# Router of a mixture-of-experts layer taken from the raw residual tile by tile, behind an output projection ordered by column halves

## What is computed

```python
x = x + jnp.einsum('blm,md->bld', y, lw['w_out'])
x = x + moe_ffn(rmsnorm(x, lw['norm_ffn_g']), ...)
...
def moe_ffn(x, wg_r, bg_r, we_r, be_r, w_gu, w_down):
    lg = (xt @ wg_r + bg_r)                      # 4 groups
    gsel = jnp.argmax(lg, axis=-1)
    le = (xt @ we_r + be_r)                      # 32 experts, 8 of each group
    tv, ti = lax.top_k(le_g, TOP_E)              # two of the chosen group
    gate = p_group * jax.nn.softmax(tv, axis=-1)
...
        return (jax.nn.silu(a) * b) @ w_down[e]  # a, b: the halves of xb @ w_gu[e]
```

## Time and profile before

| | us |
|---|---|
| three runs, median (lowest to highest) | 889.68 (887.58 to 890.31) |
| the profiled execution: own time | 888.9 |
| its span in the trace | 887.2 |
| TensorE busy | 744.4 (84%) |
| VectorE busy | 217.6 (25%) |
| DMA, mean rate over the span | 279 GB/s |

### The profile page before, as it was taken

How to read it: one execution, slowest core, us unless ns; L and a number is a source line. 1 busy time by engine, 2 the same in 40 slices (tenths; PEclk the granted TensorE clock), 3 DMA queues, 4 the chain that set the end, 5 groups by cost and what they waited for, 6 DMA issues and landing times.

```text
span 887.2 us, 10055 instructions
## 1 busy us (share of the span) xinstructions
PE 744.4 (84%) x3636; PEld 384.7 (43%) x3636; DVE 217.6 (25%) x546; ACT 138.1 (16%) x338; POOL 187.4 (21%) x186
## 2 busy tenths in 40 slices
PE   3999999979898999829999997878777787787883
PEld 3788688857666645523333332222222222222220
DVE  4331104266749332271111011001010010100110
ACT  4212413013253411101000000000000000000000
POOL 6010000160300000012233332321312313223121
PEclk9999999989997999958999999999999999999998
DMA  9742823020420194477999999999999999999992
GB/s 313 115 148 60 262 106 104 1 72 1 182 106 0 43 425 186 153 277 292 408 409 407 413 410 405 415 407 416 411 411 415 409 413 416 408 416 411 413 417 85
DMA packets 75812, 247.55 MB, mean 279 GB/s; under 512 B 24656, under 2 KB 43999, under 8 KB 51163
## 3 DMA queue, kind: packets, MB, share of 16 engines
q1 hardware_dynamic: 62625, 232.00, 66.2%
q0 software_dynamic: 11776, 8.58, 4.4%
q10 hardware_dynamic: 1378, 6.54, 1.8%
HBM read 240.99 MB, written 24.92 MB: 300 GB/s over the span
## 4 chain that ended last, share of the span: by engine, by line
PE 40%; SPq 29%; DMA 14%; DVE 11%; issue 3%; ACT 2%; POOL 0%; ACTq 0%; DVEq 0%; POOLq 0%
PE bank L1063 37%; SPq L570 20%; SPq L577 9%; DMA reg_b<-in_exp_w_gu 6%; PE bank L1066 3%; DMA reg_a<-in_exp_w_gu 3%; DMA reg_w<-in_exp_w_gu 3%; DMA reg_x<-in_x_prompt 1%; DVE reg_a L1722 1%; DVE reg_y L1973 1%; DVE reg_a L1802 1%; DVE reg_a L1712 1%; DVE reg_x L1712 0%; DVE small L1763 0%; POOL small L673 0%
## 5 line engine op out<-in xcount | busy, mean ns | idle before, releaser
L1063 PE MATMUL bank<-reg_w,reg_y 128*64 128x512 f32 (+2 forms) x512 | 136.8, 585 | 18.4 <-DMA reg_w<-in_exp_w_gu 18.4
L1063 PE MATMUL bank<-reg_a,reg_y 128*64 128x512 f32 x528 | 124.5, 607 | 22.7 <-DMA reg_a<-in_exp_w_gu 16.8
L1063 PE MATMUL bank<-reg_b,reg_y 128*64 128x512 f32 x528 | 123.4, 600 | 22.5 <-DMA reg_b<-in_exp_w_gu 16.8
L1977 DVE TENSOR_TENSOR reg_y<-reg_y,bank 128x256 f32<-128x256 f32 x32 | 13.5, 421 | 418.9 <-ACT reg_y L1046 418.9
L1063 PEld LDWEIGHTS bank<-reg_w,reg_y 128*64 128x64 f32 (+2 forms) x512 | 46.1, 146 | 103.5 <-issue 59.5
L1063 PE MATMUL bank<-reg_b,reg_w 128*128 128x260 f32 x384 | 85.3, 383 | 0.0
L1063 PEld LDWEIGHTS bank<-reg_a,reg_y 128*64 128x64 f32 x528 | 34.3, 138 | 104.2 <-issue 50.5
L1063 PEld LDWEIGHTS bank<-reg_b,reg_y 128*64 128x64 f32 x528 | 34.4, 136 | 102.4 <-issue 56.9
L1063 PEld LDWEIGHTS bank<-reg_b,reg_w 128*128 128x128 f32 x384 | 72.7, 190 | 12.0 <-issue 1.1
L673 POOL TENSOR_TENSOR small<-small 128x1 f32<-128x1 f32 (+4 forms) x18 | 20.2, 1127 | 197.2 <-DVE small L1855 68.1
L739 POOL DMA_INDIRECT out_y_p<-reg_y,reg_q x16 | 25.3, 1582 | 166.5 <-ACT reg_y L1050 166.5
(11 more groups left out here) (341 smaller groups left out, 657.1 us busy)
## 6 DMA issues: line engine op xcount, KB each, us to landing
reg_a<-in_exp_w_gu SPq DMA_DIRECT2D x44, 1024.0 KB, 27.9
reg_b<-in_exp_w_gu SPq DMA_DIRECT2D x44, 1024.0 KB, 28.7
reg_w<-in_exp_w_gu SPq DMA_DIRECT2D x40, 1024.0 KB, 27.9
reg_a<-in_exp_w_down SPq DMA_DIRECT2D x22, 1024.0 KB, 28.4
reg_b<-in_exp_w_down SPq DMA_DIRECT2D x22, 1024.0 KB, 28.1
reg_h<-in_exp_w_down SPq DMA_DIRECT2D x20, 1024.0 KB, 28.3
reg_w<-in_w_in SPq DMA_DIRECT2D x9, 1024.0 KB, 10.6
reg_w<-in_w_out SPq DMA_DIRECT2D x1, 4096.0 KB, 13.3
```

The lines of the kernel that those rows point to most:

```text
L1063: return eng.matmul(out, lhsT, rhs, start=start, stop=stop, skip_group_check=True)
L1977: tt(hid[b], silu[b], bank[2 + b][:, 256:512], ALU.mult).then_inc(S["hid_made"], 1)
```

## The change

- The output projection goes by column halves: first half 0 of all tiles, then half 1. `w_out` is loaded as two tensors, one for each half.
- There is no `h2`. TensorE turns halves of the raw `x1` as soon as they are added; `rt_w` is multiplied by the gain once, on GpSimd; the root comes in where VectorE reads the logits. Turns, logits and counts are put between chunks of the second halves.
- Squares are taken half by half; the DRAM copy `ffn_in` holds raw rows, stored after the output's own.
- The choice runs in three groups: tiles 4, 0, 1 together, then tile 2, then tile 3, each with its own count (`posA`, `posB`, `posC`), with its part of `in_slot`.
- Gathered rows are raw. The gain is multiplied in where `xe` is copied, the root in `silu`'s scale and, with the gate, in the output's scale. The table of gates has six columns of pieces in place of three.
- The gate-and-up weights are read with 4 channels to a partition in each 512 channels, before 8 in 1024; a part stays 8 KiB to a partition.
- Expert 2's down weights are asked for right behind expert 1's, its parts 0 and 1 behind `Y3.0`, 2 and 3 behind `Y3.1`.

```diff
-        gu_dram = a["exp_w_gu"].rearrange("l e (p c) n -> (l e p) c n", c=8)
+        gu_dram = a["exp_w_gu"].rearrange("l e (s p c) n -> (l e) p s c n", s=2, c=4)
...
-            eng.dma_start(w_out, a["w_out"].rearrange("l (c p) n -> p (l c) n", p=128)).then_inc(S["wout_loaded"], 16)
+            for half in range(2):
+                src = a["w_out"].rearrange("l (c p) n -> p (l c) n", p=128)[:, :, 512 * half:512 * half + 512]
+                eng.dma_start(w_out[half], src).then_inc(S["wout_loaded"], 16)
...
-            eng.dma_start(gain_ffn, a["norm_ffn_g"].rearrange("l d -> (l d)").partition_broadcast(128)).then_inc(S["gainf_loaded"], 16)
             for e in range(2):
                 load_gu(e, e)
                 load_down(e, e)
+            eng.wait_ge(S["rows_stored"], 16 * 4)
+            eng.wait_ge(bank_full[bank_of["NT3"]], turn_of["NT3"] + 1)
+            load_down(2, 2)
+            eng.wait_ge(bank_full[bank_of["Y3.0"]], turn_of["Y3.0"] + 1)
+            load_gu(2, 2, parts=(0, 1))
             eng.wait_ge(bank_full[bank_of["Y3.1"]], turn_of["Y3.1"] + 1)
-            load_gu(2, 2)
-            eng.wait_ge(S["h2_stored"], 16 * NTILE)
-            eng.wait_ge(bank_full[bank_of["hTb3"]], turn_of["hTb3"] + 1)
-            load_down(2, 2)
+            load_gu(2, 2, parts=(2, 3))
             load_experts(0)
...
+            eng.tensor_tensor(rt_w, rt_w, params[:, P_FFN_G:P_FFN_G + 8].unsqueeze(2).to_broadcast([128, KC, 36]), ALU.mult).then_inc(S["rtw_scaled"], 1)
...
-            def sums(n):
+            def square(n, half):
...
+                at = slice(512 * half, 512 * half + 512)
+                earlier = 5 + n if half and n else n + (n > 0) + half
+                if earlier >= 2:
+                    eng.wait_ge(S["x1_ss"], earlier - 1)
+                scratch = squares[0:r, 512 * (earlier % 2):512 * (earlier % 2) + 512]
+                eng.activation(scratch, x1[0:r, i, at], ACT.Square, scale=1.0 / 32, accum_out=x1_sq[0:r, n, half:half + 1]).then_inc(S["x1_ss"], 1)
...
+            square(0, 0)
+            square(0, 1)
+            x1_turned(0, 0)
+            x1_turned(0, 1)
+            store_rows(0)
+            for n in range(1, NTILE):
+                drained(eng, f"Y{TILES[n]}.0")
+                square(n, 0)
+            for n in range(1, NTILE):
+                x1_turned(n, 0)
+                drained(eng, f"Y{TILES[n]}.1")
+                square(n, 1)
+                x1_turned(n, 1)
+                store_rows(n)
...
+                eng.activation(silu[b], bank[2 + b][:, 0:256], ACT.Silu, scale=slot_scale[:, 1, bass.ds(e, 1)]).then_inc(S["silu_done"], 1)
...
+                eng.activation(y_out[b], bank[6 + b][:, :], ACT.Copy, scale=slot_scale[:, 0, bass.ds(e, 1)]).then_inc(S["y_copied"], 1)
...
-            def turn_h2(n):
...
+                    drained(eng, f"Y{i}.{k}")
+                job = f"hT{'ab'[k]}{i}"
+                ps = claim(eng, job)
+                for c in range(4):
+                    ins = turn(ps[:, c * r:(c + 1) * r], x1[0:r, i, 512 * k + 128 * c:512 * k + 128 * c + 128])
+                filled(ins, job)
+            def route(n, halves=(0, 1)):
...
+                    drained(eng, f"hT{'ab'[k]}{i}")
+                    for c in range(4 * k, 4 * k + 4):
+                        ins = mm(ps[0:r, 36 * n:36 * n + 36], h2T[:, c, 0:r], rt_w[:, c, :], c == 0, c == KC - 1)
+                    if k == 1:
+                        ins.then_inc(S["routed"], 1)
+            def positions(job, group, masks):
+                eng.wait_ge(S["mask_made"], masks)
+                ps = claim(eng, job)
+                for n in group:
+                    for k in range(n + 1):
+                        ins = mm(ps[:, 32 * n:32 * n + 32], before_bf[:, :] if k == n else ones_bf[:, :], mask_bf[:, k, :], k == 0, k == n)
+                filled(ins, job)
...
+            def project_out(n, half, between_chunks):
...
+                    if c in between_chunks:
+                        step, args = between_chunks[c]
+                        step(*args)
+                    ins = mm(ps[0:r, :], yT[:, c, COL[i]:COL[i] + r], w_out[half][:, c, :], c == 0, c == KC - 1)
...
+            for n in range(1, NTILE):
+                drained(eng, f"NT{TILES[n]}")
+                project_out(n, 0, {6: (turn_x1, (0, 0)), 7: (turn_x1, (0, 1))} if n == 1 else {3: (route, (0,))} if n == 2 else {})
+            project_out(1, 1, {4: (turn_x1, (1, 0))})
+            for n in range(2, NTILE):
+                steps = {2: (turn_x1, (n - 1, 1)), 5: (route, (n - 1,)), 7: (turn_x1, (n, 0))}
+                if n == 4:
+                    steps[4] = (positions, ("posA", range(3), 1))
+                project_out(n, 1, steps)
+            positions("posB", [3], 2)
+            route(4, [0])
+            turn_x1(4, 1)
+            route(4, [1])
+            positions("posC", [4], 3)
...
-                    ins = mm(bank[0][:, 64:160], in_slot[:, m_, :], ids[:, m_ // 5, m_ % 5, 2:5].rearrange("p f e -> p (f e)"), m_ == 0, m_ == 9)
+                    ins = mm(bank[0][:, 64:256], in_slot[:, m_ // 2, m_ % 2, :], scale_ids[:, m_ // 2, m_ % 2].rearrange("p f e -> p (f e)"), m_ == 0, m_ == 9)
...
+                by_channel = xe_rows[b].rearrange("n (p c) -> n c p", c=4)
+                for c in range(4):
+                    ins = turn(bank[1][:, 128 * c:128 * c + 128], by_channel[:, c, :])
...
+            def group_choice(g):
...
+                eng.wait_ge(S["x1_rs"], g[-1] + 1)
+                eng.wait_ge(S["routed"], g[-1] + 1)
...
+                for n in g:
+                    r = ROWS[TILES[n]]
+                    stt(lg8[0:r, n, 0:4], ps[0:r, 36 * n:36 * n + 4], rstd[0:r, n:n + 1], rt_b[0:r, 0:4], ALU.mult, ALU.add)
+                for n in g:
+                    r = ROWS[TILES[n]]
+                    ins = stt(logits[0:r, n, :], ps[0:r, 36 * n + 4:36 * n + 36], rstd[0:r, n:n + 1], rt_b[0:r, 4:36], ALU.mult, ALU.add)
...
+                for n in g:
+                    ins = eng.max(mx8[:, n, :], lg8[:, n, :])
+                link(ins)
+                for n in g:
+                    ins = eng.max_index(mi8[:, n, :].bitcast(U32), mx8[:, n, :], lg8[:, n, :])
+                link(ins)
+                at = slice(g[0], g[-1] + 1)
+                link(eng.tensor_copy(gsel[:, at], mi8[:, at, 0].bitcast(U32)))
+                eqg = ohp[:, at, 0, :]
+                link(tt(eqg, grp_iota.unsqueeze(1).to_broadcast([128, len(g), N_EXP]), wide(gsel[:, at], g, N_EXP), ALU.not_equal))
+                link(stt(eqg, eqg, NEG, logits[:, at, :], ALU.mult, ALU.add))
...
+            def expert_choice(g):
+                at = slice(g[0], g[-1] + 1)
+                eqg = ohp[:, at, 0, :]
+                for n in g:
+                    ins = eng.max(tv8[:, n, :], ohp[:, n, 0, :])
+                link(ins)
+                for n in g:
+                    ins = eng.max_index(ti8[:, n, :].bitcast(U32), tv8[:, n, :], ohp[:, n, 0, :])
+                link(ins)
+                link(eng.tensor_copy(tif[:, at, :], ti8[:, at, 0:2].bitcast(U32)))
+                for k in range(2):
+                    ins = tt(oh[:, at, k, :], exp_iota.unsqueeze(1).to_broadcast([128, len(g), N_EXP]), wide(tif[:, at, k], g, N_EXP), ALU.is_equal)
+                link(ins)
+                if g[0] == 0:
+                    link(ts(oh[:, 0], oh[:, 0], valid, None, ALU.mult))
+                tt(mask_bf[:, at, :], oh[:, at, 0, :], oh[:, at, 1, :], ALU.add).then_inc(S["mask_made"], 1)
...
+            def count_before(g, job):
...
+                for k in range(2):
+                    ins = tt(ohp[:, at, k, :], oh[:, at, k, :], cols, ALU.mult)
...
+                link(eng.tensor_reduce(pk[:, at, :], ohp[:, at], X_AXIS, ALU.add))
...
+            def find_slots(at, g):
+                lo, m_ = g[0], len(g)
+                tt(in_slot[:, lo:lo + m_].rearrange("p t k s -> p (t k) s"), cap_iota.unsqueeze(1).to_broadcast([128, 2 * m_, 2 * CAP]),
+                   at[:, lo:lo + m_].rearrange("p t k -> p (t k)").unsqueeze(2).to_broadcast([128, 2 * m_, 2 * CAP]), ALU.is_equal).then_inc(S["in_slot_made"], 1)
+            drained(eng, "Y4.0")
+            tt(x1[0:NS, 4, :], x1[0:NS, 4, :], y_smp, ALU.add).then_inc(S["x1_smp"], 1)
+            ask_rstd(0)
+            for n in range(1, NTILE):
+                add_half(n, 0)
+            for n in range(1, 3):
+                add_half(n, 1)
+                ask_rstd(n)
+            group_choice(range(3))
+            add_half(3, 1)
+            expert_choice(range(3))
+            ask_rstd(3)
+            row_ids(range(3))
+            count_before(range(3), "posA")
+            find_slots(pk, range(3))
+            group_choice([3])
+            expert_choice([3])
+            add_half(4, 1)
+            row_ids([3])
+            ask_rstd(4)
+            count_before([3], "posB")
+            find_slots(pk, [3])
+            group_choice([4])
```

(12 more changed lines are left out.)

386 lines of the change are left out of this document (156 added, 230 removed).

## The result

The changed kernel takes **879.47 us** (median of four runs, 878.70 to 881.82) against 889.61 for the kernel before in the same session (887.58 to 890.31): ratio 0.9894, 95% interval 0.9869 to 0.9919. The forecast was 879.7, the range 876 to 886. The profiled execution took 879.65, its span is 877.9 (before 888.9 and 887.2).

A forecast was written before the change was run, and what follows sets the result against it. The prediction took the second half as bound by the stream of expert weights, its end moving with the first reload. Terms 3.5 + 0.5 - 8.1 - 4.3 - 1.9 + 0.7 = -9.6 us gave 879.7 us, range 876 to 886.

The forecast's parts named there:

- product's length, with handing over: Output product: more turns, logits and a count ahead of its end, +3.5 us, and handing over at eight more places, +0.5.
- product's end to last logits: From the output product's end to the last tile's logits: 11.8 us before, 3.7 after, so -8.1 us.
- choice: Choice behind the last logits: 15 instructions for one tile, 2.7 us, in place of 7.0 for five tiles, -4.3.
- slots: Slots behind the choice: a 256-wide instruction in place of 1280-wide, count's copy gone, 3.6 us to 1.7, -1.9.
- gather and turns to first product: Ahead of expert 0's first product: gate table 192 wide in place of 96, +0.7 us; the gather keeps its length.
- first reload: Load of expert 3's weights once expert 0's first part is used: 9.6 us earlier, the end moving one for one.
- Hidden with 1.9 us to spare: Last store of rows ahead of the gather: lands behind 2 MiB of loads before the indices are there, costing nothing.
- They give nothing by themselves: Expert 2's earlier loads: fill idle DMA time without own gain, but clear the queues for the store.
- the stream's addresses: Rival: gate-and-up rows 16 KiB apart in place of 32 slow the weight stream, 5% giving 894.7 us; chance 0.06.
- no gain: Rival: the stream begins earlier but runs as much slower, or the mixers give the gain back, 889 us; chance 0.07.
- Hand-overs cost more: Rival: interleaved work holds TensorE up, the store lands late or the clock is down, 1 to 3 us each; chance 0.17.
- more than the sum: Rival: TensorE still at 2.4 GHz at expert 0, first part 1.96 us rather than 3.5, end 877 us; chance 0.10.

The follow-up runs named there:

- Table later: Changed kernel with TensorE making the table of gates behind expert 0's gate-and-up products, first six experts written out ahead of the loop: 884.82 us, ratio 0.9947.
- late gate-and-up: Changed kernel with expert 2's gate-and-up load whole behind the product, its down load left early: 883.28 us, ratio 0.9922.
- store first: Changed kernel with raw rows stored ahead of y and GpSimd's wait for y's stores moved to ahead of the first scatter: 879.19 us, ratio 0.9882.
- old rows: Changed kernel reading gate-and-up weights at the addresses of before, gathered rows keeping the new channel order (wrong pairs multiplied): 880.34 us, ratio 0.9907.

## Why the prediction was right, step by step

| step | predicted | measured |
|---|---|---|
| product's length, with handing over | +4.0 | +3.7 |
| mixers' end | 0 | +0.57 (spread of runs) |
| product's end to last logits | -8.1 | -8.35 (11.64 to 3.29) |
| choice | -4.3 | -4.2 (7.0 to 2.78) |
| slots | -1.9 | -2.2 (3.59 to 1.40) |
| slots to gather | 0 | +0.65 |
| gather and turns to first product | +0.7 | +0.49 |
| first part | 0 | -0.08 |
| first reload | -9.6 | -9.44 |

The sum came out within 0.2 us, closer than its terms did. Five of them came out better than I had them, by 1.1 us together (product, last logits, slots, gather and turns, first part), and the mixers' end, the choice and the wait for the store worse, by 1.3. The mechanism held in every step but the store; that the two sides cancel to 0.2 is luck.

- **The bound.** That the end moves one for one with the first reload held in every run but one, over a range of 14 us. "Table later" shows its limit: with the down reload of expert 0 and the one behind it over 4 us late, the end came 4.75 later.
- **Product and last logits.** The interleaved work cost what its records last, and the clock stayed at 1.00 until 377, so both halves of the last logits took 1.06 and 1.08, not the 3.63 for a whole set of before. The first group's choice ended 0.48 us ahead of the add behind it (363.76), where I had 0.6 to spare.
- **Choice.** 15 instructions in 2.78 us are 0.185 each. I had 0.18 from the rows, 2.7 in all. The formula of the Trainium skill ("VectorE: DVE Perf Modes", TRN2 errata), which gave an estimated 2.9, was about as good here.
- **Store.** "Hidden with 1.9 us to spare" is the step that failed. I let 3.15 MB move at 413 GB/s from 373.5, and the store land at 382.1. The amount was right, the rate not. One window of the changed kernel, 374 to 384, holds just these bytes, at 315 GB/s in the mean with the engines busy for 0.93 of it; the first packet moved at 374.4, the last of the stores ended at 384.0:

```profile
374.00:384.00 10.00, 3.13 (x36) 2.54 (x35) 7.66 (x47) 1.64 (x5) 0.55 (x1) 0.66 0.93 315
```

Mixing loads and stores is not slow by itself, since "late gate-and-up" moved both at 422 GB/s from 379 to 386; why it was slower here is open. So the store landed 2 us later or more, and was the releaser; it cost 0.6, which "store first" took back. The sign that the prediction named for this was there: from indices to gather 1.62 to 1.96 us in the changed kernel and four profiles like it, 1.07 to 1.09 where the indices come last.
- **Early loads.** "They give nothing by themselves" was wrong in what it led the reader to think. Without them the change gains 4 us (0.9957), not 10. The price I gave for their absence, 2.2, held only the store (3.3 measured); the down weights ahead of the gather (3.6) were in none of my terms, since before the change the chain was too slow to meet them.
- **Chances.** The rivals of the stream's addresses and of "no gain" are out by "old rows" and the table. "Hand-overs cost more" had one part right (the late store, 0.6), "more than the sum" its mechanism (the clock), which by chance comes partly true in some executions: up to 1.4 us for the first part.

## What to carry to other kernels

Where the second half is a stream of transfers, find the first one that waits for compute, and count every microsecond ahead of it, but count the transfers in front of a gather or a store too: a chain that gets shorter runs into loads that it used to outlast, and a load moved into idle time shows its worth only then. Edits that undo each other's cover must be undone singly and together; one at a time, these two seemed to be worth 11.6 us, and together they were worth 7.4. When TensorE idles ahead of a stretch that the end waits for, a few products of no use can keep its clock up: here they brought the reload 1.2 to 2.5 us nearer to the first turn. They must end before the data come. The five ahead of the gather's landing took 4.5 us at the full clock and did; at the lower clock they would take twice that, an estimate, and hold up the turns, which no run met.

## What was not expected of the hardware

- Stores on ScalarE's queue, issued behind 2 to 4 MiB of loads on SyncE's, move their first packet only 3.6 to 4.2 us after their issue (0.8 with nothing in front) and then take turns with the loads, packet for packet. The gather that waits for the last of them goes out 13.3 and 13.4 us behind its issue with 4 MiB in front, 10.1 with 2 MiB. A gather by GpSimd behind 2 MiB takes 6.73 us in place of 3.1.
- The clock of TensorE, down after the last logits, came back between 0.4 and 3.2 us behind the first product in nine profiles of the same code, which alone is 1.4 us of spread at the first reload (2.31 to 3.69 for the first part); with TensorE kept at work it stayed at 1.00 in two profiles of three.
- The start of the run spreads by 2.3 us at the product's end, so a single profile says nothing on half a microsecond there, while differences between two moments of one profile repeat within 0.15 where the clock does not come in (P to gather 11.96, 12.00, 12.02, 12.04, 12.10).
